# The last tile of the RWKV values' projection moved between the first pair's steps

## The chip, the cores and the metric

One NeuronCore of a Trainium2 chip runs the whole kernel. The metric is the device time of one execution in microseconds (us), lower is better. TensorE (PE in the rows) multiplies matrices, VectorE (DVE), ScalarE (ACT) and GpSimd (POOL) do the elementwise work, SyncE (SP) issues the transfers. Each engine takes its instructions in the order in which the program gives them, and waits at semaphores for the others.

## The reference

Two transformer blocks run one after the other on a sequence of 512 tokens with 1024 features, in float32. The change lies in the RWKV layer of the first block. Cut to what matters here:

```python
xr, xw, xk, xv, xa, xg = h[None] + xx[None] * mu[:, None, None, :]
r, k, v = jnp.einsum('nbsd,nde->nbse', jnp.stack([xr, xk, xv]), w_rkv)
w = -jax.nn.softplus(-(w0 + jnp.tanh(xw @ w1) @ w2)) - 0.5
a = jax.nn.sigmoid(a0 + (xa @ a1) @ a2)
g = jax.nn.sigmoid(xg @ g1) @ g2
...
y = _wkv7_scan(rh, decay, kh, vh, -kk, kk * ah)   # state = state*w + (state@a) b + v k
...
out = ((y + bonus).reshape(bsz, seq, d) * g) @ w_o
```

`_wkv7_scan` is a recurrence over the tokens for each of 16 heads of 64 features.

## The kernel before, in words

Activations stand transposed: 128 features of a tile on the partitions, 512 tokens along the row, 8 tiles. A float32 product is made of three products of rounded halves: weights' high with input's high (L697), weights' low with input's high (L698), weights' high with input's low (L703), each 128x128 by 128x512, for 8 blocks of the inner dimension. So a tile of a projection is 24 matmuls. The projections r, k and v run in this order, 8 tiles each; ScalarE copies each finished tile of v out of PSUM (L1261) into VV.

The scan is done in chunks of 64 tokens, and for a pair of heads (one tile of 128 features, "pair m", 8 pairs) at a time. Each pair has three kinds of step:

- "pre": 15 steps. Step 0 makes decay and rate products (TensorE L1519 and L1522) and their sigmoids (ScalarE L1617, L1620), then VectorE's running sum (L1683) and ScalarE's square (L1624); step 2 the column sums (L1529) and their reciprocal (VectorE L1688, L1690); steps 3 and 4 VectorE's L1693 to L1704 and ScalarE's exponentials; step 5 the decayed products (TensorE L1542, scaled by VectorE L1712, masked by GpSimd L1777); step 7 transposes the values (L1551, read twice by VectorE, L1718 and L1720, into VTOK); step 8 the keys' products (L1559, VectorE L1725); steps 10 to 12 further transposes and a product (L1567, L1573, L1580, L1587); step 13 the bonus (L1593, L1595); step 14 the gate (L1601 to L1608, copied by ScalarE L1667 to VV).
- "inv": the inverse of a triangular 64x64 matrix for each head and chunk: a first product (L1797, copied to TN by ScalarE L1830) and five levels. A level has a product u (L1806), VectorE's mask of it (L1839), two products (L1817 and L1823), and VectorE's two updates of TN and TT (L1844, L1847). The next level waits for them.
- "post": the state's recurrence over the 8 chunks and the output.

`rwkv_order` writes down in which order steps of the kinds of neighbouring pairs follow each other (pair m's inverse with pair m−1's post and pair m+1's pre), and `in_turn` runs this one list on every engine, so all queues have the same interleaving. Five steps of pair 0's pre are run between the tiles of v (AHEAD). The second weight of the gate (g2) is loaded by SyncE (L3188 and around), split by ScalarE (L1646, L1647) and VectorE (L1730, L1733) in pair 0's pre.

PSUM has 8 banks. In this phase they are rings that are handed out in the order of the same list: three banks for the inverse, ps3 to ps5 for pre and post, ps6, ps7 and ps5 for pair 0's first products. A product that takes a bank waits until its last user has been read.

## Time and profile before

| what | value |
|---|---|
| median of 3 runs | 2939.98 us |
| the three runs | 2934.58, 2939.98, 2943.99 us |
| the profiled execution | 2940.94 us, its span 2939.2 us |
| mean granted TensorE clock | 0.982 of full |
| TensorE busy | 2836.8 us, 97% of the span |
| VectorE, ScalarE, GpSimd busy | 1573.0, 1038.1, 189.2 us |

The span runs from the first to the last instruction of the profiled execution; the time holds what lies around it too. Times in the rows below count from the span's start. The stretch of this change begins near 738 us; the scan runs until about 1047 us.

### The profile page before, as it was taken

Reading aid. Unit: us, or ns where it says so; the run is one execution under the profiler, and the core shown is the slowest. Engines: PE = TensorE matmul, PEld = TensorE weight load, DVE = VectorE, ACT = ScalarE, POOL = GpSimd, SP = SyncE. Lnnn points to the kernel's source line nnn. Section 1 sums busy time; section 2 is a strip of 40 time slices with the busy share of each in tenths; the row PEclk is TensorE's granted clock in tenths of the full one; section 3 lists DMA queues with packets and bytes.
Section 4 is the critical chain, followed back from the end, with each engine's and each line's share of the span. In section 5 each row is a group of like instructions: output and inputs, shape, how many; then the busy total and the mean of one; then the engine's idle time right before and its main releaser. Section 6 shows DMA issues by size and latency. Waiting matters only on the chain.

```text
span 2939.2 us, 44934 instructions
## 1 busy us (share of the span) xinstructions
PE 2836.8 (97%) x20056; PEld 2296.9 (78%) x20056; DVE 1573.0 (54%) x2214; ACT 1038.1 (35%) x1338; POOL 189.2 (6%) x167
## 2 busy tenths in 40 slices
PE   7999999999899989999999999899999998999999
PEld 5878888778788878888777777688888786788887
DVE  7766544464677753233466666454344646454342
ACT  4235234353333235233432322242223447532221
POOL 0010000101322110000100000010000000100000
PEclk9999999999999999999999999799999999999999
DMA  7544554221000032222211111032322220222322
GB/s 276 227 172 174 199 200 171 81 86 44 17 3 3 17 115 101 100 101 93 76 58 44 44 44 44 1 115 78 116 92 88 91 82 1 89 98 79 115 83 68
DMA packets 41377, 270.78 MB, mean 92 GB/s; under 512 B 4576, under 2 KB 4832, under 8 KB 13280
## 3 DMA queue, kind: packets, MB, share of 16 engines
q1 hardware_dynamic: 40752, 266.37, 25.1%
q8 instruction: 157, 2.57, 0.3%
q10 hardware_dynamic: 432, 1.54, 0.1%
q14 instruction: 36, 0.29, 0.0%
HBM read 265.80 MB, written 2.10 MB: 91 GB/s over the span
## 4 chain that ended last, share of the span: by engine, by line
PE 88%; DVE 8%; ACT 3%; issue 1%; DMA 1%; SPq 0%; POOL 0%; DVEq 0%; ACTq 0%
PE ps L697 21%; PE ps L703 21%; PE ps L698 21%; PE ps L2276 6%; PE ps L3054 1%; PE ps L1823 1%; PE ps L1817 1%; PE ps L2382 1%; PE ps L1806 1%; PE ps L2441 1%; DVE WL L409 1%; PE ps L2435 1%; PE ps L2410 1%; PE ps L2971 1%; PE ps L2958 1%
## 5 line engine op out<-in xcount | busy, mean ns | idle before, releaser
L697 PE MATMUL ps<-HH,WH 128*128 128x512 f32 x1928 | 766.5, 398 | 19.4 <-ACT HH L673 16.6
L698 PE MATMUL ps<-HH,WL 128*128 128x512 f32 x1928 | 756.4, 392 | 0.0
L703 PE MATMUL ps<-HL,WH 128*128 128x512 f32 x1928 | 730.7, 393 | 4.9 <-DVE HL L909 3.6
L409 DVE TENSOR_TENSOR WL<-ST,WH 128x2048 fp32r<-128x2048 f32 (+3 forms) x230 | 465.1, 2023 | 230.8 <-ACT WH L401 230.7
L401 ACT ACTIVATE WH<-ST 128x2048 fp32r<-128x2048 f32 (+1 forms) x211 | 384.1, 1820 | 310.0 <-PE ps L703 281.6
L697 PEld LDWEIGHTS ps<-HH,WH 128*128 128x128 f32 x1928 | 365.4, 190 | 102.9 <-issue 23.5
L703 PEld LDWEIGHTS ps<-HL,WH 128*128 128x128 f32 x1928 | 364.5, 189 | 85.8 <-DVE HL L909 5.8
L698 PEld LDWEIGHTS ps<-HH,WL 128*128 128x128 f32 x1928 | 365.7, 190 | 78.6 <-issue 3.8
L698 PE MATMUL ps<-GH,WL 128*128 128x512 f32 x928 | 361.4, 389 | 0.0
L697 PE MATMUL ps<-GH,WH 128*128 128x512 f32 x928 | 361.4, 389 | 0.0
L703 PE MATMUL ps<-GL,WH 128*128 128x512 f32 x928 | 360.0, 389 | 0.0
L698 PEld LDWEIGHTS ps<-GH,WL 128*128 128x128 f32 x928 | 174.3, 188 | 36.2
L703 PEld LDWEIGHTS ps<-GL,WH 128*128 128x128 f32 x928 | 174.3, 188 | 36.1
L697 PEld LDWEIGHTS ps<-GH,WH 128*128 128x128 f32 x928 | 174.2, 188 | 36.0
L749 DVE SCALAR_TENSOR_TENSOR X<-ps,MOD,X 128x512 f32<-128x512 f32 (+1 forms) x52 | 36.3, 707 | 196.4 <-PE ps L703 196.4
L1016 DVE TENSOR_TENSOR GL<-TMP,GH 128x512 fp32r<-128x512 f32 x64 | 44.3, 692 | 169.0 <-ACT GH L1009 167.4
L532 POOL TENSOR_TENSOR ACC<-ACC,TMP 128x512 f32<-128x512 f32 x43 | 56.8, 1321 | 1059.9 <-ACT TMP L521 1050.8
L2276 PE MATMUL ps<-HH,WH 128*128 128x512 f32 x256 | 118.1, 461 | 0.0
L2276 PE MATMUL ps<-HL,WH 128*128 128x512 f32 x256 | 103.2, 403 | 0.0
L2276 PE MATMUL ps<-HH,WL 128*128 128x512 f32 x256 | 102.7, 401 | 0.0
L454 DVE CUSTOM_DVE_ANT_0 ADA<-ST,CROW,CC 128x1024 f32<-128x1024 f32 x80 | 102.5, 1318 | 0.0
L752 DVE TENSOR_TENSOR X<-X,ps 128x512 f32<-128x512 f32 x48 | 32.6, 685 | 129.7 <-PE ps L703 129.7
(408 smaller groups left out, 3519.0 us busy)
## 6 DMA issues: line engine op xcount, KB each, us to landing
ST<-w_m SPq DMA_DIRECT2D x64, 1024.0 KB, 4.8
ST<-w_gu SPq DMA_DIRECT2D x44, 1024.0 KB, 4.8
ST<-w_ada SPq DMA_DIRECT2D x40, 1024.0 KB, 5.7
ST<-w_dn SPq DMA_DIRECT2D x32, 704.0 KB, 4.1
ST<-w_gin SPq DMA_DIRECT2D x16, 1024.0 KB, 4.8
ST<-w_cin SPq DMA_DIRECT2D x12, 1024.0 KB, 4.9
ST<-w_rkv SPq DMA_DIRECT2D x12, 1024.0 KB, 4.8
W<-w_ada SPq DMA_DIRECT2D x16, 512.0 KB, 16.9
```

The lines of the kernel that those rows point to most:

```text
L401: e.activation(WH[:, j % 3, 0:n], ST[:, pos % 3, 0:n], ACT.Copy).then_inc(*hi.up(j))
L409: o = e.tensor_tensor(WL[:, j % 3, cut], ST[:, pos % 3, cut], WH[:, j % 3, cut].bitcast(F32), ALU.subtract)
L454: e.tensor_tensor_reduce(out=ADA[:, 2 * d:2 * d + 2, :], in0=tile, in1=CROW[:, :].rearrange("p (a b) -> p a b", a=2), scale=1.0, scalar=co ...
L532: e.tensor_tensor(sums_of(t)[:, :], sums_of(t)[:, :], tmp.tile(("square", t, k)), ALU.add).then_inc(*sumsq.up(t, k))
L697: e.matmul(ps[:, :], wh[:, k, cs], H[:, k, :], start=(k == 0), stop=False)
L698: e.matmul(ps[:, :], wl[:, k, cs], H[:, k, :], start=False, stop=False)
L703: o = e.matmul(ps[:, :], wh[:, k, cs], L[:, k, :], start=False, stop=(k == kt - 1))
L749: e.scalar_tensor_tensor(out=X[:, m, cs], in0=ps[:, cs], scalar=gcol(m), in1=X[:, m, cs], op0=ALU.mult, op1=ALU.add).then_inc(*res.up(tag, ...
L752: e.tensor_tensor(X[:, m, :], X[:, m, :], ps[:, :], ALU.add).then_inc(*res.up(tag, m))
L1016: e.tensor_tensor(GL[:, m, :], tmp.tile((tag, m)), GH[:, m, :].bitcast(F32), ALU.subtract).then_inc(*out_vec.up(tag, m))
L1806: o = e.matmul(ps[rows(hh), 64 * c:64 * c + 64], BG[b][rows(hh), c, 128:192], TN[rows(hh), c, :], start=True, stop=True)
L2276: o = e.matmul(ps[:, :], a[:, k, c0:c0 + P], b[:, k, :], start=(k == 0 and part == 0), stop=(k == KT - 1 and part == 2))
```

## The change

The last tile of v (tile 7) leaves the projection (`but=7`) and is made in eight steps of its own, kind "v", one for each block of the inner dimension, which `rwkv_order` puts between the steps 5 to 14 of pair 0's pre. Pair 1's pre step 0 comes before pair 0's bonus, in front of the inverse's first product; pair 0's gate product goes behind pair 1's step 8, and two of pair 1's steps behind the first level of the inverse. The split of the gate weights is now a kind of its own, "gates", two steps. Waits for tile 7 become waits for tile 6, and the instructions that need tile 7's end wait for it themselves; the load of g2 is issued behind tile 6.

```diff
@@ tensor_dense
-                for group in ([tiles] if n == 0 else [[m] for m in tiles]):
+                for group in ([tiles] if n == 0 else [[m] for m in tiles if m != but]):
@@ rwkv_order
-            out = [("pre", 0)] * PRE
+            a, b, v = ("pre", 0), ("pre", 1), ("v", 7)
+            out = [a] * AHEAD + [v, v, a, a, v, a, v, v, a, a, v, a, a, v, a, v, b, a, b]
...
-                    steps += [(moved("pre", i, PRE), 2, "pre", m + 1) for i in range(PRE)]
+                    steps += [(moved("pre", i, PRE), 2, "pre", m + 1) for i in range(0 if m else 2, PRE)]
                 steps = [(kind, n) for _, _, kind, n in sorted(steps)]
+                if m == 0:
+                    steps[3:3] = [steps.pop(2)]
+                    steps[13:13] = [a]
+                    steps[8:8] = [("gates", 0)]
+                    steps[5:5] = [("gates", 0)]
@@ scalar_pre
-                if m == 0 and i == 6:
-                    e.wait_ge(s_g2, 16)
-                    e.activation(G2H[:, :], LG2[:, 0, :], ACT.Copy).then_inc(*scan_act.up("g2 high"))
-                    e.activation(G2B, LG2[0:96, 1, :], ACT.Copy).then_inc(*scan_act.up("g2 tail"))
@@ vector_pre
+            if m == 1:
+                e.wait_ge(*mm.at("v", 7))
...
-            if m == 0:
-                e.wait_ge(*scan_act.at("g2 high"))
-                e.tensor_tensor(G2L[:, :], LG2[:, 0, :], G2H[:, :].bitcast(F32),
-                                ALU.subtract).then_inc(*scan_vec.up("g2 low"))
-                e.wait_ge(*scan_act.at("g2 tail"))
-                e.tensor_tensor(G2B[32:64, :], LG2[32:64, 1, :], G2B[32:64, :].bitcast(F32),
-                                ALU.subtract).then_inc(*scan_vec.up("g2 tail"))
@@ pool_pre
+            if m == 1:
+                e.wait_ge(*mm.at("v", 7))
+                e.tensor_tensor(RI[1][:, 0, :, :], over(tb("idk"), 8), over(tb("idk"), 8),
+                                ALU.mult).then_inc(*scan_pool.up("identity"))
@@ new functions
+        def tensor_value(e, m):
+            for k in range(KT):
+                tensor_group(e, "v", 3, [m], k, HH, HL, None, None, first_b)
+                yield
+
+        def scalar_value(e, m):
+            for k in range(KT - 1):
+                yield
+            e.wait_ge(*mm.at("v", m))
+            e.activation(VV[:, m, :], first_b.tile(("v", m))[:, :], ACT.Copy).then_inc(*out_act.up("v", m))
+            e.wait_ge(s_tab, 16)
+            e.activation(BONES, tb("bones"), ACT.Copy).then_inc(*scan_act.up("bones"))
+            yield
+
+        def scalar_gates(e, _):
+            e.wait_ge(*mm.at("v", 7))
+            e.wait_ge(s_g2, 16)
+            e.activation(G2H[:, :], LG2[:, 0, :], ACT.Copy).then_inc(*scan_act.up("g2 high"))
+            e.activation(G2B, LG2[0:96, 1, :], ACT.Copy).then_inc(*scan_act.up("g2 tail"))
+            while True:
+                yield
+
+        def vector_gates(e, _):
+            yield
+            e.wait_ge(*scan_act.at("g2 high"))
+            e.tensor_tensor(G2L[:, :], LG2[:, 0, :], G2H[:, :].bitcast(F32),
+                            ALU.subtract).then_inc(*scan_vec.up("g2 low"))
+            e.wait_ge(*scan_act.at("g2 tail"))
+            e.tensor_tensor(G2B[32:64, :], LG2[32:64, 1, :], G2B[32:64, :].bitcast(F32),
+                            ALU.subtract).then_inc(*scan_vec.up("g2 tail"))
+            while True:
+                yield
@@ tensor_rwkv (the other engines alike)
-            e.wait_ge(*out_act.at("v", 7))
+            e.wait_ge(*out_act.at("v", 6))
@@ SyncE
-                    e.wait_ge(*mm.at("v", 7))
+                    e.wait_ge(*mm.at("v", 6))
                     e.dma_start(LG2[:, :, :], lo2[:, 1:3, :]).then_inc(s_g2, 16)
```

The list of steps decides the rest, so here is what stands on the engines. Line numbers of the changed kernel are larger by 16 around the pre steps of TensorE (L1542 is L1558 there, L1551 is L1567, L1559 is L1575, L1519 is L1535) and by 11 in the inverse (L1806 is L1817, L1817 is L1828, L1823 is L1834).

TensorE before, at the end of the values' projection; the last three matmuls of tile 7 and pair 0's step 5:

```order
L697 MATMUL ps<-HH,WH 128x512
L698 MATMUL ps<-HH,WL 128x512
L703 MATMUL ps<-HL,WH 128x512
L1542 MATMUL ps<-RI_104,BP 64x128 [waits scan_pool,scan_vector,out_activated]
L1542 MATMUL ps<-RI_104,BP 64x128 x15
L1551 MATMUL ps<-TB,VV 128x128 x4
```

TensorE of the changed kernel at the same place; the first row is tile 7's first matmul:

```order
L697 MATMUL ps<-HH,WH 128x512 [waits out_activated]
L698 MATMUL ps<-HH,WL 128x512
L703 MATMUL ps<-HL,WH 128x512
L697 MATMUL ps<-HH,WH 128x512
L698 MATMUL ps<-HH,WL 128x512
L703 MATMUL ps<-HL,WH 128x512
L1558 MATMUL ps<-RI_104,BP 64x128 [waits scan_pool,scan_vector]
L1558 MATMUL ps<-RI_104,BP 64x128 x15
L697 MATMUL ps<-HH,WH 128x512
```

Tile 7 has two of its eight steps ahead of step 5 and six behind; tile 6's copy is what its first matmul waits for. This is TensorE of the changed kernel where tile 7 ends and pair 1 begins:

```order
L697 MATMUL ps<-HH,WH 128x512
L698 MATMUL ps<-HH,WL 128x512
L703 MATMUL ps<-HL,WH 128x512
L1535 MATMUL ps<-ADA,LO_81 128x512 [waits scan_vector]
L1538 MATMUL ps<-ADA,LO_81 128x512 [waits scan_activated]
L1609 MATMUL ps<-RKH,HH 128x512 [waits scan_activated]
L1611 MATMUL ps<-RKL,HH 128x512 [waits scan_pool]
L1808 MATMUL ps<-TB,TT_99 64x64 [waits scan_pool]
L1808 MATMUL ps<-TB,TT_99 64x64 x15
L1817 MATMUL ps<-TN,BG_89 64x64 [waits scan_activated]
L1817 MATMUL ps<-TN,BG_89 64x64 x15
L1828 MATMUL ps<-UN,TT_99 64x64 [waits scan_vector]
```

Pair 1's two products (L1535, L1538) and the bonus (L1609, L1611) stand ahead of the inverse's first product (L1808); before, the inverse's product stood ahead of pair 1's. The column sums (L1529, now L1545) were ahead of level 1's two products and are behind them.

VectorE before, first where the gate weights are split (L1730, L1733), in pair 0's pre:

```order
L1725 TENSOR_TENSOR GK_91<-ps,TB 128x4x128
L1730 TENSOR_TENSOR G2L<-LG_86,G2H 128x1024 [waits scan_activated]
L1733 TENSOR_TENSOR HL<-LG_86,HL 32x1024 [waits scan_activated]
L1736 TENSOR_TENSOR BG_89<-ps,TINY 128x8x64 [waits scan_summed]
L1740 TENSOR_TENSOR TT_99<-BG_89,TB_82 128x512 [waits scan_pool]
```

and then around the second level of pair 0's inverse (mask L1839, updates L1844 and L1847), with pair 1's L1712 between:

```order
L1704 SCALAR_TENSOR_TENSOR T_109<-RR,CC,KK 128x512 [waits scan_vector]
L1839 TENSOR_TENSOR UN<-ps,TB_82 128x512 [waits scan_summed]
L1712 TENSOR_TENSOR BG_93<-ps,TINY 128x4x128 [waits scan_summed]
L1844 TENSOR_TENSOR TN<-TN,ps 128x512 [waits scan_summed]
L1847 TENSOR_TENSOR TT_99<-TT_99,ps 128x512 [waits scan_summed]
```

VectorE of the changed kernel around the second level (mask L1850, gate weights L2078 and L2081, updates L1855 and L1858):

```order
L1850 TENSOR_TENSOR UN<-ps,TB_82 128x512 [waits scan_summed]
L1726 TENSOR_TENSOR BG_93<-ps,TINY 128x4x128 [waits scan_summed]
L2078 TENSOR_TENSOR G2L<-LG_86,G2H 128x1024 [waits scan_activated]
L2081 TENSOR_TENSOR HL<-LG_86,HL 32x1024 [waits scan_activated]
L1855 TENSOR_TENSOR TN<-TN,ps 128x512 [waits scan_summed]
L1858 TENSOR_TENSOR TT_99<-TT_99,ps 128x512 [waits scan_summed]
```

The two subtractions of the gate weights have gone from pair 0's pre to between the mask and the update of level 2.

TensorE before around the third level, with bank numbers: transposed values of pair 1, its keys' products, the level's two products:

```order
L1551 MATMUL ps4<-TB_58,VV_74 128x128 x4
L1559 MATMUL ps5<-RI1_105,KP_108 64x128 [waits scan_vector,scan_pool]
L1559 MATMUL ps3<-RI1_105,KP_108 64x128
...
L1817 MATMUL ps2<-UN_102,TT0_99 64x64 [waits scan_vector]
L1817 MATMUL ps2<-UN_102,TT0_99 64x64 x15
L1823 MATMUL ps0<-TT0_99,UN_102 64x64 x16
```

TensorE of the changed kernel at the same place:

```order
L1567 MATMUL ps3<-TB_58,VV_74 128x128 x4
L1575 MATMUL ps4<-RI1_105,KP_108 64x128 [waits scan_vector,scan_pool]
L1575 MATMUL ps3<-RI1_105,KP_108 64x128
...
L1617 MATMUL ps5<-GAH_78,G2H_88 128x512 [waits scan_activated]
L1619 MATMUL ps5<-GAL_79,G2H_88 128x512 [waits out_vector]
L1621 MATMUL ps5<-GAH_78,G2L_87 128x512
L1624 MATMUL ps5<-GBH_80,HL_51 128x512 [waits out_vector]
L1828 MATMUL ps2<-UN_102,TT0_99 64x64 x16
L1834 MATMUL ps0<-TT0_99,UN_102 64x64 x16
```

Pair 0's gate product (L1617 to L1624) now stands between the keys' products and the level's products. The transposed values are in ps3, which the keys' products use too; before they were in ps4, which these did not use.

## Rows read from the trace of the kernel before

**Rows 1.** The page: granted clock by slices, and the chain that ended last.
```profile
PEclk9999999999999999999999999799999999999999
...
PE 88%; DVE 8%; ACT 3%; issue 1%; DMA 1%; SPq 0%; POOL 0%; DVEq 0%; ACTq 0%
```

**Rows 2.** Time line, TensorE: start us, us, engine, line, operation, count, [idle before].
```profile
725.93 0.95 PE L1529 MATMUL ps<-TB,ACC 128*128 128x2 f32 x8
...
737.74 0.39 PE L697 MATMUL ps<-HH,WH 128*128 128x512 f32 x1
...
742.96 0.39 PE L703 MATMUL ps<-HL,WH 128*128 128x512 f32 x1
744.03 1.59 PE L1542 MATMUL ps<-RI,BP 64*64 64x128 f32 x32 [0.69 <-ACT VV L1261]
...
756.44 0.69 PE L1519 MATMUL ps<-ADA,LO 64*128 64x512 f32 x1
...
757.50 1.15 PE L1806 MATMUL ps<-TN,BG 64*64 64x64 f32 x32
```

**Rows 3.** Busy time by stretch; first a line of columns.
```profile
core 0: us, PE busy (x) PEld busy (x) DVE busy (x) ACT busy (x) POOL busy (x), PEclk, DMA share, GB/s
744.03:756.44 12.41, 9.43 (x150) 7.47 (x151) 8.99 (x12) 4.40 (x7) 6.06 (x5) 1.00 0.25 86
765.00:767.00 2.00, 2.00 (x38) 1.83 (x35) 1.62 (x3) 0.00 (x0) 1.50 (x2) 0.50 0.00 0
775.00:790.00 15.00, 14.87 (x345) 12.38 (x338) 8.96 (x15) 3.58 (x6) 2.73 (x3) 1.00 0.01 3
```

**Rows 4.** Time line, TensorE, pair 0's inverse.
```profile
761.60 1.05 PE L1529 MATMUL ps<-TB,ACC 128*128 128x2 f32 x8 [2.95 <-ACT ACC L1624]
762.58 1.15 PE L1817 MATMUL ps<-UN,TT 64*64 64x64 f32 x32
763.56 1.75 PE L1823 MATMUL ps<-TT,UN 64*64 64x64 f32 x32
...
772.40 1.15 PE L1806 MATMUL ps<-TN,BG 64*64 64x64 f32 x32
...
776.05 1.10 PE L1823 MATMUL ps<-TT,UN 64*64 64x64 f32 x32
...
782.71 1.15 PE L1806 MATMUL ps<-TN,BG 64*64 64x64 f32 x32
...
784.65 1.15 PE L1823 MATMUL ps<-TT,UN 64*64 64x64 f32 x32
```

**Rows 5.** Time line, VectorE.
```profile
727.70 0.69 DVE L1695 SCALAR_TENSOR_TENSOR KK<-ACC,KK 128x512 f32<-128x512 f32 x1
...
750.10 1.29 DVE L1730 TENSOR_TENSOR G2L<-LG,G2H 128x1024 fp32r<-128x1024 f32 x1
...
752.67 0.69 DVE L1736 TENSOR_TENSOR BG<-ps,TINY 128x512 f32<-128x512 f32 x1
...
766.81 0.69 DVE L1695 SCALAR_TENSOR_TENSOR KK<-ACC,KK 128x512 f32<-128x512 f32 x1
...
768.02 1.78 DVE L1704 SCALAR_TENSOR_TENSOR T<-RR,CC,KK 128x512 f32<-128x512 f32 x1
769.73 0.68 DVE L1839 TENSOR_TENSOR UN<-ps,TB 128x512 f32<-128x512 f32 x1
...
771.66 0.69 DVE L1844 TENSOR_TENSOR TN<-TN,ps 128x512 f32<-128x512 f32 x1 [0.65 <-PE ps L1817]
...
775.11 0.69 DVE L1720 SCALAR_TENSOR_TENSOR VTOK<-TINY,ps 128x512 f32<-128x512 f32 x1
...
783.90 0.69 DVE L1839 TENSOR_TENSOR UN<-ps,TB 128x512 f32<-128x512 f32 x1 [0.98 <-PE ps L1806]
```

**Rows 6.** Time line, GpSimd.
```profile
767.65 1.61 POOL L1773 TENSOR_TENSOR KP<-KK,TMP 128x512 f32<-128x512 f32 x1 [1.15 <-DVE KK L1695]
```

**Rows 7.** Source line L1704: duration ns min/median/max, first and last start.
```profile
L1704 DVE SCALAR_TENSOR_TENSOR T<-RR,CC,KK x8: 737/740/1794, 729.8 to 977.1; 128x512 f32<-128x512 f32 x8
```

More of the change, by code:

```diff
@@ L707, in tensor_group, with tensor_dense @@
                     o.then_inc(*took.up(tag, k))
-        def tensor_dense(e, tag, H, L, high, low, after=None, hooked=True, begun=(0,), norm=None, first=0):
+        def tensor_dense(e, tag, H, L, high, low, after=None, hooked=True, begun=(0,), norm=None, first=0, but=None):
             for n, j in enumerate(J[tag]):
@@ L1164, in plan_projections @@
                     for m in (2 * n, 2 * n + 1):
-                        big.use((tag, m), out_act, tag, m)
+                        if (tag, m) != ("v", 7):
+                            big.use((tag, m), out_act, tag, m)
             return ahead(plan_pre)
@@ L1219, in tensor_projections @@
                 tensor_dense(e, tag, HH, HL, split_high("mix" + tag), split_low("mix" + tag),
-                             lambda m: next(pre) if 1 < m < 2 + AHEAD else None, tag == "v")
+                             lambda m: next(pre) if 1 < m < 2 + AHEAD else None, tag == "v",
+                             but=7 if tag == "v" else None)
             return {("pre", 0): pre}
@@ L1259, in scalar_projections @@
                             scalar_split(e, "mix" + then, None, (tag, 7), tag)
+                        if (tag, m) == ("v", 7):
+                            continue
                         e.wait_ge(*mm.at(tag, m))
@@ L1506, in plan_wo, with plan_value @@
                 yield
+        def plan_value(m):
+            first_b.use(("v", m), out_act, "v", m)
+            while True:
+                yield
         def plan_rwkv(begun):
-            in_turn(RWKV, {"pre": plan_pre, "inv": plan_inv, "post": plan_post, "wo": plan_wo}, begun)
+            in_turn(RWKV, {"pre": plan_pre, "inv": plan_inv, "post": plan_post, "wo": plan_wo, "v": plan_value,
+                           "gates": no_value}, begun)
             plan_residual("wo", "mlp1")
@@ L1878, in tensor_post @@
             e.wait_ge(*scan_act.at("kt", m))
+            if m == 0:
+                e.wait_ge(*out_act.at("v", 7))
             if m:
@@ L2038, in scan_low, with no_value @@
             return scan_vec.at("low", k)
+        def tensor_value(e, m):
[25 more added lines that the diff above has]
+                            ALU.subtract).then_inc(*scan_vec.up("g2 tail"))
+            while True:
+                yield
+        def no_value(m):
+            while True:
+                yield
         def tensor_rwkv(e):
             begun = tensor_projections(e)
-            e.wait_ge(*out_act.at("v", 7))
+            e.wait_ge(*out_act.at("v", 6))
             in_turn(RWKV, {"pre": lambda m: tensor_pre(e, m), "inv": lambda m: tensor_inv(e, m),
-                           "post": lambda m: tensor_post(e, m), "wo": lambda n: tensor_wo(e, n)}, begun)
+                           "post": lambda m: tensor_post(e, m), "wo": lambda n: tensor_wo(e, n),
+                           "v": lambda m: tensor_value(e, m), "gates": no_value}, begun)
             tensor_dense(e, "wo", HH, HL, scan_high, scan_low, begun=(7,))
@@ L2057, in vector_rwkv @@
             begun = vector_projections(e)
-            e.wait_ge(*mm.at("v", 7))
-            e.wait_ge(*out_act.at("v", 7))
+            e.wait_ge(*mm.at("v", 6))
+            e.wait_ge(*out_act.at("v", 6))
             in_turn(RWKV, {"pre": lambda m: vector_pre(e, m), "inv": lambda m: vector_inv(e, m),
-                           "post": lambda m: vector_post(e, m), "wo": lambda n: vector_wo(e, n)}, begun)
+                           "post": lambda m: vector_post(e, m), "wo": lambda n: vector_wo(e, n),
+                           "v": no_value, "gates": lambda _: vector_gates(e, _)}, begun)
             vector_low(e, J["wo"][1])
@@ L2075, in pool_rwkv @@
                 next(begun["pre", 0])
-            e.wait_ge(*mm.at("v", 7))
-            e.wait_ge(*out_act.at("v", 7))
-            e.tensor_tensor(RI[1][:, 0, :, :], over(tb("idk"), 8), over(tb("idk"), 8), ALU.mult)
+            e.wait_ge(*mm.at("v", 6))
+            e.wait_ge(*out_act.at("v", 6))
             in_turn(RWKV, {"pre": lambda m: pool_pre(e, m), "inv": lambda m: iter(()), "post": lambda m: iter(()),
-                           "wo": lambda m: iter(())}, begun)
+                           "wo": lambda m: iter(()), "v": no_value, "gates": no_value}, begun)
             pool_squares(e, "mlp1")
```

7 lines of the change are left out of this document (3 added, 4 removed).

## The prediction, on record before the result

> **What bounds the kernel now.** I read the page first. The chain that ended last lies on TensorE for 88% of the span and on VectorE for 8% [rows 1]: what counts is when TensorE can start, and an edit gains only what it takes out of TensorE's gaps. Two numbers bound this edit. A tile of the values' projection is 24 matmuls, from 737.74 to 742.96 in starts, 0.227 us apart, so 5.44 us [rows 2]. And between the first step of pair 0 behind it (744.03) and the first of pair 1 (756.44) TensorE is busy for 9.43 of 12.41 us at the full clock [rows 2, 3]: 2.98 us are gaps. In front of 744.03 stand 0.69 us more, for ScalarE's copy of tile 7; a copy of tile 6 will be waited for in the same way, so that gap stays.
>
> Then I read on down TensorE's order of time. After 757.50 it stands for 2.95 us until 761.60, for ScalarE (table load, sigmoids, VectorE's scan, the square) [rows 4]. In 765 to 767 the granted clock is 0.50, the 1.2 GHz level; before it fell TensorE had been idle up to 761.60 and then ran 64-column matmuls [rows 3, 4]. From 775 to 790 it is busy for 14.87 of 15 us [rows 3]: what is late at 776.05, the second product of pair 0's third level, is late for good, and what is early there stays early. So 776.05 is the point at which I settle the account. Every later pair repeats an order of instructions that the change leaves alone.
>
> **The change, part by part.** The work is the same: no matmul, copy or transfer is added, the identity product on GpSimd only comes later. The sum is one of times.
>
> *1. The tile between pair 0's steps.* TensorE starts at 744.03 − 5.44 = 738.6, with two steps of the tile. To pair 1's first product (L1519) it then has the 9.43 us, less what is now put behind it: four gate matmuls (4 × 0.23 = 0.9), the two of the bonus (0.6) and the inverse's first product (about 1.0, the distance of two such groups at 762.58 and 763.56 [rows 4]), plus 5.44 of the tile: 9.43 − 2.5 + 5.44 = 12.4 us, to within half a us: L1519 at 751.0 for 756.44, so 5.4 earlier. The gaps are filled; VectorE's copies, for which they were, end behind the steps of the tile.
>
> *2. Pair 1's first steps.* Behind L1519 come ScalarE's table load and sigmoids, VectorE's scan and ScalarE's square, and TensorE could use the square 761.60 − 756.44 = 5.16 us behind L1519 [rows 2, 4], so at 756.2. ScalarE now does all this first and only then copies the inverse's first product (about 0.55 more, estimated from the other plain steps between engines here). The first level (L1806) starts at 756.7, against 757.50. Most of the 5.4 is gone here: the 2.95 us gap has moved ahead of L1806. The column sums (L1529), which waited for the square, now stand behind level 1: one level takes 1.94 to its second product (782.71 to 784.65), the two products about 1.0 each [rows 4]; so L1529 starts at 756.7 + 1.94 + 2.0 = 760.6. From L1529 to KK's update (L1695) pair 0 took 727.70 − 725.93 = 1.77 [rows 2, 5], and from there to level 2's mask (L1839) it is 769.73 − 766.81 = 2.92 [rows 5]. L1839: 760.6 + 1.77 + 2.92 = 765.3 for 769.73, 4.4 earlier.
>
> *3. The gate weights.* On VectorE L1730 and L1733 take 752.67 − 750.10 = 2.57 us [rows 5]. There they filled time in which TensorE stood anyway; now they stand directly ahead of level 2's update (L1844), for which level 3 waits on TensorE. L1844 follows L1839 by 1.93, of which the time line shows 0.65 idle, so by 1.28 of work; with the 2.57 it is 3.85: 769.15 for 771.66, 2.5 earlier. Then the port. The mask on GpSimd (L1777) now runs beside these two. KP's product on GpSimd (767.65, 1.61 us) and L1704 on VectorE (768.02, 1.78 us) overlap in this trace; L1704 reads two tiles of SBUF and takes 0.74 as a rule [rows 5 to 7]. If L1730 or L1733 is held in the same way, up to 1.05 is added; if GpSimd is the one held, nothing. Nearest is L1704, but here VectorE is first; I take 0.6. Left: 1.9 earlier at level 3 (772.40 becomes 770.5). ScalarE's two copies (G2H, G2B) cost nothing: it has no work between the exponentials and RKH. SyncE issues their load behind tile 6, not 7, and nothing is queued behind it until the gates of pair 7; GpSimd's identity product waits for tile 7 (751.2 in the new order) and takes GpSimd's place only while that waits for pair 1's sigmoids anyway.
>
> The Trainium skill (GPSIMD Engine Reference, section 1 Specifications) says that GpSimd's SBUF interfaces are shared with VectorE and that contention comes with instructions of two SBUF inputs. By that rule both gate subtractions are exposed and the full 1.05 would be due, 0.45 more than I take; L1704 agrees with it.
>
> *4. A new wait in the ring of PSUM tiles.* This is what the diff doesn't show and the order with tile numbers does: before, pair 1's transposed values go to ps4, and the decayed keys' product (L1559) to ps5 and ps3. Now both use ps3, so L1559 waits until VectorE has read the values twice (L1718, L1720). Before, L1720 started at 775.11, 2.7 behind level 3's start, and nobody waited. Now the mask on level 3's product (L1839) stands ahead, which starts 1.2 behind the product (782.71 to 783.90 [rows 4, 5]), then 0.6 of the mask, 0.7 of the sum L1718 and 0.7 of L1720 itself: L1559 can start 3.2 behind level 3. It then takes 1.5 (the like group at 744.03, 1.59 on its row, of which the last 0.1 lies under the next [rows 2]), the gate matmuls of pair 0, now behind it, 0.95 to 1.1, the first product 1.0. So the second product starts 6.75 behind level 3; before it was 776.05 − 772.40 = 3.65. That is 3.1 later.
>
> **Sum:** 1.9 earlier at level 3, 3.1 later behind it: 1.2 us later at 776.05, and as much at the end. Against the profiled execution (2940.94, of which 2939.2 is span) this gives 2942.1; its time is 1 us above the median of the three runs, 2939.98, so by the median **2941.2 us**. Bounds: without the port (−0.6), with the gate matmuls at 0.9 and L1559's tail beside the next group (−0.7) it is −0.1; with the full port (+0.45) and half the clock for one level's products, which took 1.75 for 1.15 at 763.56 [rows 4] and would now touch column sums too (+1.2), it is +2.9. This case's own range is 2939.9 to 2942.9, to which the runs' scatter, 2934.58 to 2943.99, is to be added.
>
> **Rivals.**
> (a) *The gain is kept.* If L1559 doesn't wait for L1720 in effect, or the gate subtractions slip into VectorE's idle time, 2 to 5.4 us stay: 2934.5 to 2938. For it: 2.98 us of gaps are really filled. Against: the order on VectorE is fixed, and the tile numbers are. It decides at level 3: this case needs it over 3.1 us earlier. Chance 0.27, middle 2937.
> (b) *TensorE's clock.* Level 1 to 3 now has gaps of about 2.8, 0.7, 1.1, 1.0 and 1.6 us in 20. If the whole of it runs at 1.2 GHz, some 8.6 us of products on the path (two a level, sums, keys, gates) take twice as long: 2941.2 + 8.6 = 2950, slower by over 0.3%. Against: 0.50 was granted here for some 3 us only. It decides when over 7.5 us of the products are at half clock. Chance 0.06 for that much.
> (c) *The clock elsewhere.* The page's PEclk shows a slice at 7 behind the middle [rows 1]: far from the change, and 0.3 of a slice of 73.5 us is some 22 us of clock. A shift by a few us may change its length either way. If a third of it goes, 2934; half, 2930. Chance 0.12, split over both signs.
> The Trainium skill (TensorE: Matmul & The Clock Gate, "Why this matters for your kernels") advises against idle gaps between bursts because the clock falls back. By that rule (b) would be likelier before than after, since the longest gap is 2.95 and would be about 2.8; no run here yet shows it.
>
> **How the numbers follow.** Forecast (0 to 3 us slower) 0.55, (a) 0.27, (b) 0.06, (c) 0.12. A measurement of this kernel can tell about 0.3%, 8.8 us, from no change; neither the forecast nor (a) reaches that, since the tile's 5.44 us are the most that can be had. So within 0.3%: 0.55 + 0.27 + most of (c) = 0.89; slower by more 0.06, from (b); faster by more 0.05, from (c). The range 2935 to 2946 holds the forecast and (a) with part of the scatter.
>
> **What the profile after would show.** L1542's first group at about 738.6 + 1.5; L1519 of pair 1 at 751.0; L1806 at 756.7 behind a wait for TN of nearly 3 us; the level 2 update on VectorE directly behind L1733's row, at 769 to 770; L1559 of pair 1 with a wait of 1 to 2 us for VTOK; L1823 of level 3 at 776 to 778.5. I am wrong if L1559 doesn't wait there, if level 3 starts before 769, or if the time from there to the end of the scan differs from that of before.

## The result and the profile after

The changed kernel takes **2946.74 us** (median of 22 runs, 2938.09 to 2957.99) and the kernel before 2939.26 us (22 runs, 2933.21 to 2944.74). The medians differ by 7.5 us. The ratio over all runs is 1.0031, with a 95% interval of 1.0023 to 1.004: slower by 0.31%. The forecast was 2941.2, in a range of 2935 to 2946; the median lies just above it. The profiled execution of the changed kernel took 2945.96 us, of which 2944.2 are its span, 5.0 us more than that of before.

The page of the changed kernel gives the first hint, against [rows 1]:

```profile
PEclk9999999999899999999999999799999999999999
...
PE 88%; DVE 8%; ACT 3%; issue 1%; DMA 1%; SPq 0%; DVEq 0%; ACTq 0%
```

TensorE still holds 88% of the chain. In the middle a slice of PEclk stands at 7 in both. But there is a new 8, the eleventh slice, that is 736 to 810 us: just where the change is. The time line of TensorE of that stretch, with the columns of [rows 2]:

```profile
750.03 0.69 PE L1535 MATMUL ps<-ADA,LO 64*128 64x512 f32 x1
...
755.68 1.98 PE L1817 MATMUL ps<-TN,BG 64*64 64x64 f32 x32 [2.77 <-ACT TN L1841]
758.45 1.97 PE L1828 MATMUL ps<-UN,TT 64*64 64x64 f32 x32 [0.79 <-DVE UN L1850]
...
765.28 2.61 PE L1558 MATMUL ps<-RI,BP 64*64 64x128 f32 x30 [1.10 <-DVE RI L1715]
...
772.97 1.97 PE L1817 MATMUL ps<-TN,BG 64*64 64x64 f32 x32 [2.78 <-DVE TN L1855]
...
777.58 2.89 PE L1575 MATMUL ps<-RI,KP 64*64 64x128 f32 x32 [1.60 <-DVE VTOK L1734]
780.40 0.79 PE L1617 MATMUL ps<-GAH,G2H 128*128 128x512 f32 x1
...
783.40 1.10 PE L1834 MATMUL ps<-TT,UN 64*64 64x64 f32 x32
```

I read it against [rows 2, 4]. Everything is counted from tile 6's last matmul, 737.51 before and 736.71 now, so that what happened earlier in the execution drops out.

| from tile 6's last matmul, us | before | after | forecast of the difference | measured |
|---|---|---|---|---|
| pair 1's first product (L1519, now L1535) | 18.93 | 13.32 | −5.4 | −5.61 |
| level 1 starts (L1806, now L1817) | 19.99 | 18.97 | −0.8 | −1.02 |
| level 3 starts | 34.89 | 36.26 | −1.9 | +1.37 |
| level 3's second product (L1823, now L1834), called D below | 38.54 | 46.69 | +1.2 | +8.15 |
| last copy of the scan on ScalarE, called S below | 304.89 | 312.90 | as D | +8.01 |

Up to level 1 the forecast holds to 0.2 us. Then 2.4 us come on until level 3, and 6.8 in level 3. From there to the end of the scan nothing changes any more (8.15 and 8.01). In the rows one sees why: L1817 (L1806 before) took 1.15 and takes 1.98 at 755.68 and 1.97 at 772.97; L1828 (L1817 before) takes 1.97 at 758.45 for 1.15, and L1575 2.89 at 777.58, for the 1.59 of the like group at 744.03. The granted clock of the changed kernel, by stretches (the columns are those of [rows 3]):

```profile
core 0: us, PE busy (x) PEld busy (x) DVE busy (x) ACT busy (x) POOL busy (x), PEclk, DMA share, GB/s
...
750.00:755.00 5.00, 2.90 (x39) 1.61 (x38) 1.92 (x2) 3.88 (x7) 2.11 (x2) 1.00 0.00 0
755.00:760.00 5.00, 3.53 (x61) 3.34 (x62) 0.69 (x1) 4.97 (x8) 2.37 (x3) 0.52 0.01 3
760.00:765.00 5.00, 4.18 (x80) 3.91 (x78) 3.17 (x7) 0.09 (x1) 0.81 (x2) 0.80 0.00 0
765.00:770.00 5.00, 4.72 (x96) 4.72 (x96) 4.32 (x5) 0.63 (x1) 2.41 (x2) 0.66 0.02 5
770.00:775.00 5.00, 2.22 (x41) 1.97 (x36) 4.07 (x5) 0.00 (x0) 1.93 (x2) 0.72 0.00 0
775.00:780.00 5.00, 3.40 (x34) 3.03 (x36) 2.06 (x3) 0.00 (x0) 1.68 (x2) 0.50 0.02 3
...
738.00:790.00 52.00, 42.96 (x684) 36.34 (x683) 27.50 (x39) 13.36 (x21) 17.79 (x13) 0.80 0.07 22
```

Two of the same stretches of the kernel before:

```profile
775.00:780.00 5.00, 5.00 (x149) 4.71 (x142) 4.59 (x9) 0.60 (x1) 1.47 (x2) 1.00 0.01 3
738.00:790.00 52.00, 43.40 (x806) 36.13 (x806) 29.53 (x43) 16.64 (x26) 16.74 (x13) 0.97 0.07 22
```

The clock is full until 755. Level 1 runs at 0.52 (the 1.2 GHz level), then it is mixed from 760 to 775, and from 775 to 780 it is at 0.50 again. Read in stretches of half a microsecond, it is at the low level three times: from about 755.2 to 762.0, 765.4 to 768.8 and 772.2 to 782.5. Ahead of each TensorE stood idle: 2.77 us before 755.68, for TN, 1.10 us before 765.28, for RI, and 2.78 us before 772.97, for TN again. Over the 52 us it was granted 0.80 for 0.97. It was busy about as long (42.96 and 43.40 us) with 684 instructions instead of 806, so it got less done in the same busy time. The ends of matmuls are modelled, so busy time alone does not show this; the starts do.

VectorE and GpSimd around the gate weights, against [rows 5, 6]:

```profile
768.78 1.22 DVE L2078 TENSOR_TENSOR G2L<-LG,G2H 128x1024 fp32r<-128x1024 f32 x1
770.03 2.17 DVE L2081 TENSOR_TENSOR HL<-LG,HL 32x1024 fp32r<-32x1024 f32 x1
772.22 0.69 DVE L1855 TENSOR_TENSOR TN<-TN,ps 128x512 f32<-128x512 f32 x1
```

```profile
768.94 2.17 POOL L1788 TENSOR_TENSOR BG<-BG,TB 128x512 f32<-128x512 f32 x1 [2.59 <-DVE BG L1726]
774.19 1.27 POOL L1788 TENSOR_TENSOR BG<-BG,TB 128x512 f32<-128x512 f32 x1 [3.07 <-DVE BG L1726]
```

The first subtraction takes 1.22, the second 2.17 us. Together they last from 768.78 to 772.22, 3.44 us for the 2.57 of before. GpSimd's mask beside them needs 2.17 instead of the 1.27 that it takes at 774.19. That is the contention for which the forecast took 0.6. By the starts and ends the two engines look as if they took turns: the mask starts 0.16 behind the first subtraction, which takes its usual time (1.22, and 1.29 before), and ends 1.11 behind that one's end; the second subtraction ends 1.09 behind the mask's end.

### The profile page after: what moved, and what is told of

It is laid out like the page before. It is cut to its first block, busy times and chain, and to the rows that moved or that the text cites. A ratio compares the mean times of both kernels' runs of the same rounds, so it can differ in the third digit from the quotient of the medians.

```text
span 2944.2 us, 44934 instructions
## 1 busy us (share of the span) xinstructions
PE 2840.9 (96%) x20056; PEld 2299.9 (78%) x20056; DVE 1574.0 (53%) x2214; ACT 1037.9 (35%) x1338; POOL 190.4 (6%) x167
## 3 DMA queue, kind: packets, MB, share of 16 engines
q8 instruction: 157, 2.57, 0.4%
## 4 chain that ended last, share of the span: by engine, by line
PE 88%; DVE 8%; ACT 3%; issue 1%; DMA 1%; SPq 0%; DVEq 0%; ACTq 0%
PE ps L697 21%; PE ps L703 21%; PE ps L698 21%; PE ps L2326 6%; PE ps L3104 1%; PE ps L1834 1%; PE ps L1828 1%; PE ps L1817 1%; PE ps L2432 1%; PE ps L2491 1%; DVE WL L409 1%; PE ps L2485 1%; PE ps L2460 1%; PE ps L3021 1%; PE ps L3008 1%
```

## The experiments

Each kernel ran 12 times, in turn with the kernel before (median 2939.2 to 2939.5 in all three comparisons); the last was run once. D and S are defined above and come from one profiled execution each. "Rest" is the span less the end of the scan, so the part of the program in which no kernel here differs from another. "Clock" is the granted clock of 738 to 790 us.

| kernel | median (range), us | ratio to before, 95% | D | S | clock | rest |
|---|---|---|---|---|---|---|
| before | 2939.26 (2933.21 to 2944.74) | | 38.54 | 304.89 | 0.97 | 1896.8 |
| changed | 2946.74 (2938.09 to 2957.99) | 1.0031, 1.0023 to 1.004 | 46.69 | 312.90 | 0.80 | 1894.6 |
| e1_fill_after | 2939.15 (2932.14 to 2943.78) | 1.0, 0.9989 to 1.0011 | 40.25 | 306.66 | 1.00 | 1893.0 |
| e2_fill_before | 2940.32 (2933.79 to 2948.03) | 1.0008, 0.9994 to 1.0022 | 38.68 | 304.99 | 1.00 | 1894.0 |
| e3_ring | 2944.32 (2935.08 to 2954.08) | 1.0014, 0.9999 to 1.0029 | 42.59 | 310.03 | 0.84 | 1904.4 |
| e4_gates | 2941.79 (2932.31 to 2949.57) | 1.0008, 0.9996 to 1.0021 | 40.74 | 307.00 | 0.90 | 1904.3 |
| e5_inv_first | 2942.8 (2932.53 to 2954.88) | 1.0014, 1.0 to 1.0028 | 40.86 | 307.21 | 0.93 | 1894.0 |
| e6_all | 2934.88 (2930.48 to 2940.89) | 0.9986, 0.9975 to 0.9997 | 36.44 | 303.98 | 0.93 | 1890.8 |
| e7_reorder | 2936.89 (2932.9 to 2943.59) | 0.9992, 0.9981 to 1.0003 | 35.02 | 304.39 | 0.93 | 1890.6 |
| e8_fill_first | 2940.79 (2935.16 to 2954.37) | 1.0002, 0.9986 to 1.0017 | 40.16 | 306.46 | 1.00 | 1904.3 |
| e9_tile_only | 2942.28 (2937.96 to 2949.89) | 1.0015, 1.0003 to 1.0028 | 42.08 | 308.49 | 0.90 | 1890.6 |
| e10_all_fill | 2941.03 (2933.75 to 2945.09) | 1.0003, 0.9992 to 1.0014 | 35.67 | 303.15 | 1.00 | 1904.3 |
| e11_fill_rest | 2942.4 (2934.04 to 2945.17) | 1.0003, 0.9992 to 1.0015 | 42.81 | 309.15 | 0.93 | 1895.8 |
| e12_again | 2936.84 (one run) | | 45.02 | 311.21 | 0.87 | 1887.8 |

The rest varies by 17 us between executions and hides what the order is worth, so a median can tell the changed kernel from before but hardly the experiments from each other. What the stretch costs is read from D and S. Two rows show where the rest gets its differences, 1500 to 1900 us of e6_all and then of e10_all_fill:

```profile
1500.00:1900.00 400.00, 386.78 (x3631) 275.89 (x3625) 255.00 (x552) 116.90 (x174) 14.08 (x14) 0.95 0.11 38
```

```profile
1500.00:1900.00 400.00, 388.88 (x3544) 277.90 (x3540) 249.30 (x538) 115.83 (x171) 14.07 (x14) 0.91 0.11 38
```

The granted clock is 0.95 in one and 0.91 in the other, of 400 us; 0.04 of 400 is 16 us of clock, against 13.5 us in the rest.

### The clock or the order

**e1_fill_after** puts products that compute nothing into TensorE's gaps: matmuls of HH into a bank that nobody reads then. They keep TensorE running and change nothing else of the work.

```diff
+        def tensor_fill(e, n):
+            for _ in range({1: 12, 2: 3, 3: 4, 4: 8, 5: 6}[n]):
+                e.matmul(PY[:, :], HH[:, 1, 0:P], HH[:, 2, :], start=True, stop=True)
+            while True:
+                yield
...
+                    for at_, n in ((14, 5), (12, 4), (8, 3), (2, 2), (1, 1)):
+                        steps[at_:at_] = [("fill", n)]
```

> The changed kernel with 33 dummy matmuls (128x512, read from two unused places of HH, written to a free PSUM bank) in TensorE's five gaps between pair 0's first inverse product and pair 1's keys' products: 12, 3, 4, 8 and 6 of them. They do no useful work and wait for nothing. Measure D: from tile 6's last matmul to the second product of level 3, 38.5 us before, 46.7 in the changed kernel. Theory (clock): the order of instructions costs about 1 us, the other 7 are TensorE at 1.2 GHz between the gaps; with the gaps filled the granted clock stays near 1.00, D is 39.5 to 41.5 and the time about 2941, 5 to 7 us under the changed kernel. Rival (order): the new waits themselves cost it; D stays at 45 or more (the dummies can only add) and the time at 2946 or more.

TensorE's level 3 in e1_fill_after, and its clock:

```profile
773.33 1.59 PE L1577 MATMUL ps<-RI,KP 64*64 64x128 f32 x32 [0.22 <-DVE VTOK L1736]
...
776.96 1.10 PE L1836 MATMUL ps<-TT,UN 64*64 64x64 f32 x32
```

```profile
738.00:790.00 52.00, 50.41 (x835) 40.68 (x836) 30.00 (x43) 15.38 (x25) 17.91 (x13) 1.00 0.06 22
```

The clock is full over the whole stretch, and D is 40.25 for 46.69. So **6.4 of the 8.15 us are the clock, and 1.7 are the order.** The median says the same: 2939.15, 7.6 below the changed kernel and within its interval equal to before; the intervals of the two ratios (0.9989 to 1.0011 and 1.0023 to 1.004) don't meet. More work on TensorE, 33 matmuls of 128x512, made the changed kernel faster.

**e2_fill_before** does the same to the kernel before, so that its own 0.50 in 765 to 767 [rows 3] goes.

```diff
+                if m == 0:
+                    for at_, n in ((10, 4), (9, 3), (4, 1)):
+                        steps[at_:at_] = [("fill", n)]
```

(12, 4 and 3 matmuls in fills 1, 3 and 4.)

> The kernel before with 19 such dummy matmuls in its own gaps there: 12 before pair 1's column sums (the 2.95 us gap), 4 and 3 in the two gaps of about 1 us at 767 and 770. Theory (clock): the stretch at half clock from 763 to 767 vanishes; on the path that was one product of 1.5 for 0.95 us, so D goes from 38.5 to 37.5 to 38 and the time down by 0.5 to 1 us, which is less than these rounds can tell; the profile decides. Rival (order): D stays 38.5 or grows by what the dummies overrun.

The clock is 1.00 for 0.97, and D stays: 38.68 for 38.54. The gain of 0.5 to 1 us that I expected does not come. The rows of VectorE and GpSimd show why, first of before, then of e2_fill_before:

```profile
765.31 1.19 POOL L1768 TENSOR_TENSOR RI<-RR,T 128x512 f32<-128x512 f32 x1
765.95 0.82 DVE L1693 TENSOR_SCALAR ACC<-XX,CC 128x512 f32<-128x512 f32 x1
```

```profile
764.75 1.20 POOL L1775 TENSOR_TENSOR RI<-RR,T 128x512 f32<-128x512 f32 x1
764.75 1.48 DVE L1700 TENSOR_SCALAR ACC<-XX,CC 128x512 f32<-128x512 f32 x1
```

Counted from the column sums (761.60 and 761.03), VectorE comes to this step 0.63 us earlier at full clock. But beside GpSimd's product it now takes 1.48 us for 0.82, and ends 0.3 us behind GpSimd's end in both kernels. So the half clock was on the path for 0.6 us, and GpSimd's product would have held VectorE in its place. The clock of before has nothing to give back at this place, and that of the changed kernel has.

### Which gap

**e8_fill_first** fills only the gap ahead of level 1, with 12 matmuls; **e11_fill_rest** all but that one (3, 4, 10 and 6).

```diff
# e8_fill_first
+                    steps[1:1] = [("fill", 1)]
# e11_fill_rest
+                    for at_, n in ((14, 5), (12, 4), (8, 3), (2, 2)):
+                        steps[at_:at_] = [("fill", n)]
```

> The changed kernel with 12 dummy matmuls in the first gap alone (2.77 us, behind the inverse's first product). Theory (each long gap lets the clock fall again): the clock stays 1.00 to about 770 and falls behind the second gap of 2.78 us ahead of level 3, so that level 3's product, keys' and gate products keep their half clock; D 43 to 44.5, time 2943 to 2945. Rival (the first gap alone starts it): D about 40.5, time 2941, as with all gaps filled.

TensorE in e8_fill_first (L2095 is the fill), and its clock:

```profile
751.99 3.02 PE L2095 MATMUL ps<-HH 128*128 128x512 f32 x12
754.94 1.15 PE L1818 MATMUL ps<-TN,BG 64*64 64x64 f32 x32
...
769.07 1.15 PE L1818 MATMUL ps<-TN,BG 64*64 64x64 f32 x32 [2.56 <-DVE TN L1856]
...
772.42 1.59 PE L1576 MATMUL ps<-RI,KP 64*64 64x128 f32 x32 [1.62 <-DVE VTOK L1735]
...
776.06 1.10 PE L1835 MATMUL ps<-TT,UN 64*64 64x64 f32 x32
```

```profile
765.00:770.00 5.00, 2.44 (x84) 2.30 (x80) 4.94 (x5) 0.00 (x0) 2.18 (x1) 1.00 0.00 0
...
738.00:790.00 52.00, 45.09 (x817) 36.61 (x817) 29.98 (x43) 15.53 (x25) 17.85 (x13) 1.00 0.05 20
```

The clock stays full, though two gaps are left, 2.56 and 1.62 us, and TensorE is busy for 2.44 us only in 765 to 770. My expectation, that each gap takes the clock down on its own, was wrong for this execution. What differs from the changed kernel is that TensorE had not been at half clock before. That is no explanation, though. In e5_inv_first (below) the clock was at 0.50 until 765.6, TensorE stood idle for 3.01 us from 767.2, and it came back at full clock:

```profile
770.24 1.15 PE L1818 MATMUL ps<-TN,BG 64*64 64x64 f32 x32 [3.01 <-DVE TN L1856]
```

And in e6_all and e7_reorder (below too) the clock was full from 750 on and fell at a later gap, of 2.85 and 3.06 us.

Since here nothing is slowed, this profile also shows the order by itself: level 3 starts at 769.07, 33.17 behind tile 6's last matmul (735.90), 1.7 earlier than before, and its second product is 6.99 behind it. The forecast had 1.9 and 6.75.

> The changed kernel with all its gaps filled but the first, the counterpart of e8_fill_first, where the first alone was filled and the clock stayed at 1.00 (D 40.2) although gaps of 2.56 and 1.62 us were left. Theory formed from that (the first gap, behind which the first level's small products come, is what the clock answers): low clock from about 755 for some 6 us, D 42 to 44. Rival (any of the gaps does it, and e8_fill_first's one profile was lucky): also low behind the first gap, but then e8's median should not be as good as e1's, and D here is about 42 all the same; what tells them apart is whether the second half (770 to 782) stays at 1.00 here.

TensorE in e11_fill_rest, and its clock:

```profile
754.72 1.97 PE L1819 MATMUL ps<-TN,BG 64*64 64x64 f32 x32 [2.77 <-ACT TN L1843]
...
774.93 1.59 PE L1577 MATMUL ps<-RI,KP 64*64 64x128 f32 x32 [0.22 <-DVE VTOK L1736]
...
778.56 1.10 PE L1836 MATMUL ps<-TT,UN 64*64 64x64 f32 x32
```

```profile
755.00:760.00 5.00, 5.00 (x69) 4.13 (x68) 0.69 (x1) 4.11 (x6) 2.41 (x2) 0.50 0.02 3
...
765.00:770.00 5.00, 4.29 (x99) 3.81 (x96) 4.97 (x5) 0.63 (x1) 2.90 (x2) 1.00 0.02 5
...
775.00:780.00 5.00, 5.00 (x116) 4.37 (x118) 1.67 (x3) 0.60 (x1) 0.32 (x1) 1.00 0.01 3
```

The gap of 2.77 us is back, and behind it the clock is at 0.50 for one stretch, full after 765. D is 42.81, 2.6 more than with all gaps filled. So in these profiles the first gap costs 2.6 of the 6.4 us, and the later low stretches 3.9. Among the changed kernel, e8_fill_first and e11_fill_rest they came only where the first gap and their own were open together. With one profile of each kernel this does not show that they need both.

**e12_again** is the changed kernel once more, in a single run.

> The changed kernel once more, for one look: whether the half clock recurs at the same places. Theory (the fall is caused by the gaps): low again in most of 755 to 782, D 44 to 48. Rival (a chance of the one profile): 1.00 there, D about 40.

Level 3 in e12_again, and its clock:

```profile
771.73 1.61 PE L1817 MATMUL ps<-TN,BG 64*64 64x64 f32 x32 [2.57 <-DVE TN L1855]
```

```profile
770.00:775.00 5.00, 2.65 (x36) 2.13 (x36) 4.12 (x6) 0.00 (x0) 2.04 (x2) 0.72 0.00 0
```

The clock in 755:760 is 0.51 again, in 770:775 0.72 and in 775:780 0.60; only 765:770, 0.66 in the first profile, is at 1.00. D is 45.02, 1.7 less. The low stretches at level 1 and level 3 come again, the one at level 2 does not. So the same instructions with the same gap of 1.10 us ahead of level 2 ran at half clock in one execution and at full clock in the other. And ahead of level 3 the clock had been full since 762.0 when the gap of 2.57 us began at 769.2, and it fell all the same (at 772.2, 0.5 us behind the gap's end), while in e8_fill_first it held over 2.56. The two differ in the low stretch at level 1, but by e5_inv_first, e6_all and e7_reorder that does not decide either. Each profile is one case of something that varies. Its whole time is 2936.84, 10 below the median, although its D is bad: the rest is 1887.8, the shortest of all.

### Which part of the change makes the gaps

Each undoes one part in the order of steps.

```diff
# e3_ring: the gate product behind pair 1's step 8, out of level 3
-                    steps[13:13] = [a]
+                    steps[15:15] = [a]
# e4_gates: the gate weights early, in level 1
-                    steps[8:8] = [("gates", 0)]
-                    steps[5:5] = [("gates", 0)]
+                    steps[2:2] = [("gates", 0)]
+                    steps[1:1] = [("gates", 0)]
# e5_inv_first: the inverse's first product ahead of pair 1's step 0
-            out = [a] * AHEAD + [v, v, a, a, v, a, v, v, a, a, v, a, a, v, a, v, b, a, b]
+            out = [a] * AHEAD + [v, v, a, a, v, a, v, v, a, a, v, a, a, v, a, v, ("inv", 0), b, a, b]
+                    steps.pop(0)
```

> The changed kernel with pair 0's gate product two steps later (behind pair 1's step 9), so that the banks are handed out otherwise and pair 1's keys' products no longer use the bank of its transposed values. The wait of 1.60 us for VTOK goes. Rival (order): D 46.7 becomes 44.5 to 45.1, the wait and up to half a us of the gate product. Theory (clock): the same and more, since one gap fewer lets the clock return earlier: keys' products and gate product took 4.8 us at half clock for 2.5; D 42 to 44.5, time 2942 to 2945.

> The changed kernel with the split of the gate weights earlier: ScalarE's two copies behind the copy of the inverse's first product, VectorE's two subtractions behind level 1's mask, instead of between level 2's mask and its update. Level 2's update then follows its products; the gap of 2.78 us before level 3 shrinks to under 0.5. Rival (order): D 46.7 becomes 43 to 44 (2.57 of subtractions and 0.95 of port less, 0.5 more at level 1). Theory (clock): the same and also the clock of level 3, keys' and gate products (about 4 us lost there) back: D 39 to 41.5, time 2939 to 2942.

> The changed kernel with the inverse's first product ahead of pair 1's first products, as in the kernel before, so that ScalarE copies it before it loads its table, and level 1's product needn't wait for pair 1. D (tile 6's last matmul to level 3's second product) was 38.5 before, 46.7 in the changed kernel, 40.25 with its gaps filled. Theory (the 2.77 us gap ahead of level 1 lets the clock fall, order costs 1.7 us in all): the gap goes, level 1 starts 3 us earlier, D 37.5 to 41, time 2936 to 2941. Rival (the clock falls in any case in this stretch of small products, whatever the order): D 43 or more, time 2943 or more.

Level 3 in e3_ring:

```profile
774.16 1.97 PE L1817 MATMUL ps<-TN,BG 64*64 64x64 f32 x32 [2.77 <-DVE TN L1855]
...
777.11 2.25 PE L1575 MATMUL ps<-RI,KP 64*64 64x128 f32 x26
...
780.51 1.10 PE L1834 MATMUL ps<-TT,UN 64*64 64x64 f32 x32
781.53 0.50 PE L1617 MATMUL ps<-GAH,G2H 128*128 128x512 f32 x1
```

and in e4_gates:

```profile
769.74 1.15 PE L1817 MATMUL ps<-TN,BG 64*64 64x64 f32 x32
...
773.28 1.59 PE L1575 MATMUL ps<-RI,KP 64*64 64x128 f32 x32 [1.81 <-DVE VTOK L1734]
...
776.92 1.10 PE L1834 MATMUL ps<-TT,UN 64*64 64x64 f32 x32
```

e3_ring: the keys' product (L1575) starts 2.95 behind level 3 and waits for nothing, for 4.61 in the changed kernel, and the gate product (L1617) stands behind the level. The second product comes 6.35 behind level 3 instead of 10.43, and D is 4.1 less. So the wait for VTOK does hang on the gate product's place in the ring. The gap of 2.77 us ahead of level 3 stays, and with it the low clock at its start. e4_gates: the gap ahead of level 3 is gone, and the products of level 3 run in 1.15 and 1.10. GpSimd's mask no longer runs beside the two subtractions there: the second takes 1.22 for 2.17, and the mask 1.27 for 2.17. The product of GpSimd that now overlaps the second one (L1776) takes 1.85 for its 1.27. So the contention moves along with what runs side by side. The wait for VTOK stays at 1.81. D is 5.95 less. e5_inv_first: the wait ahead of level 1 is gone, one of 2.21 us for VectorE's mask comes a product later, and D is 5.8 less. In all three D lies where the clock theory had it (42 to 44.5, 39 to 41.5, 37.5 to 41). None of the three is resolved by its median from before (1.0008 to 1.0014).

**e9_tile_only** moves only the tile. Pair 1's steps stand as before, and the gate weights are split as early as tile 7 allows.

```diff
+            out = [a] * AHEAD + [kinds[c] for c in "vvaavavvaavaavavGaGa"]
+                    steps = [kinds[c] for c in "ibbibibbibibibbibibbibibib"]
```

(a and b are pre steps of pair 0 and 1, v the tile, G the gate weights, i the inverse.)

> One part alone: tile 7's steps between pair 0's steps as in the changed kernel, but the gate weights split directly behind tile 7, the gate product and everything of pair 1 in the order of the kernel before. D is 38.5 before and 46.7 in the changed kernel. Theory (the split can't start before tile 7 has read its inputs, so that the tile's 5.4 us of cover come back as a wait for the gate weights in front of the gate product): TensorE waits some 3 us there, D 38 to 40 at full clock and up to 43 if the clock falls behind that wait, time 2939 to 2944. Rival (the tile alone brings its 3 us of gaps): D 35.5 to 36.5, time 2936 to 2937.

D is 42.08, 3.5 worse than before, although the 5.44 us of the tile fill the gaps. The split of the gate weights overwrites HL, which tile 7 still reads, so it can only come behind tile 7. TensorE then waits 0.97 us ahead of the bonus, for ScalarE's copies behind tile 7, and 1.04 and 0.84 us in the gate product, for the two subtractions: 2.85 us, where the gaps of before were 2.98. So the gap that the tile fills comes back behind it. The wait ahead of the column sums stays (2.65 us for 2.95). The clock is at 0.90 in that stretch, so a part of the 3.5 is the clock again; how much, no run with fills tells. The ratio, 1.0015 (1.0003 to 1.0028), says slower too.

### The three together, and the best order

**e6_all** has the edits of e3, e4 and e5 at once; **e7_reorder** is an order written by hand, with the inverse as early as it can go; **e10_all_fill** is e6_all with 9, 4 and 11 matmuls of fill (the 4 and the 11 came to stand together, ahead of level 2).

```diff
# e7_reorder
+            out = [a] * AHEAD + [kinds[c] for c in "vvaavavvaavaavavibaib"]
+                    steps = [kinds[c] for c in "ibbGibibbGibbibaibbibibib"]
# e10_all_fill, on e6_all
+                    for at_, n in ((7, 3), (6, 2), (3, 1)):
+                        steps[at_:at_] = [("fill", n)]
```

> The inverse's first product ahead of pair 1 (as e5), the gate weights split early (as e4) and the gate product behind step 9 (as e3), together. Theory (each gap is removed where it arises): D 34 to 38, clock mostly 1.00 from 751 to 785, time 2934 to 2939. Rival (clock falls anyway): D 40 or more.

> As e6, but pair 1's scan behind level 1's mask on VectorE, level 2's product and mask ahead of its two last exponent products, and VectorE's gate subtractions behind both of pair 1's decayed products. Theory: the inverse's chain runs ahead of pair 1's, D 33 to 37, time 2933 to 2938. Rival (pair 1's own chain of ScalarE, VectorE and GpSimd bounds the stretch): D within 0.5 of e6's.

> e6_all with dummy matmuls in its three remaining gaps (9 ahead of level 1's two products, 4 ahead of level 2, 11 ahead of pair 1's decayed products). e6_all had D 36.4 with the clock at 0.54 in 765 to 770. Theory (the clock is what e6_all still loses): D 35 to 36, time 2934 to 2935. Rival (its gaps are too few for the clock to cost): D 36.4 or more.

TensorE in e6_all:

```profile
757.03 1.15 PE L1829 MATMUL ps<-UN,TT 64*64 64x64 f32 x32 [2.21 <-DVE UN L1851]
...
765.27 2.68 PE L1559 MATMUL ps<-RI,BP 64*64 64x128 f32 x30 [2.85 <-DVE RI L1716]
...
774.01 1.10 PE L1835 MATMUL ps<-TT,UN 64*64 64x64 f32 x32
```

Level 1 has moved into the time of the sigmoids, and its second product (L1829) waits 2.21 us there. D is 36.44, 2.1 less than before, and S 0.9 less. The median, 2934.88, is 12 us below the changed kernel and the only one whose interval lies below 1 (0.9975 to 0.9997, 1 to 7 us faster than before); 0.9 (by S) to 2.1 us (by D) of that are the stretch's, what is left may be the rest's. e7_reorder has the best D, 35.02, and gives back part of it by S (304.39). e10_all_fill has a clock of 1.00 and the best S, 303.15, but a median of 2941.03, where I had expected 2934 to 2935. Its profiled rest is 13.5 us longer than that of e6_all. Whether the fills bring this about, or chance, stays open.

## Why the prediction was wrong

*Part 1, the tile: right.* L1535 came 5.6 us earlier against 5.4.

*Part 2, pair 1's first steps: right.* L1817 waits 2.77 us for TN, "nearly 3" as forecast, and level 1 starts 1.0 earlier against 0.8. That the gap only moves was right; what it does to the clock at its new place was missed. Before, the clock fell behind that gap too, for the last product of level 1 and the first of level 2, and that cost nothing in the end (e2_fill_before). Now level 1's first product follows the gap directly, and all of level 1 ran at the low level.

*Part 3, the gate weights: right in size.* The contention added 0.95 us (L2081 at 2.17 against 1.22), where I took 0.6 of 0 to 1.05. It held both engines, since GpSimd's mask also took 0.9 longer; I had thought of it as one or the other. It did not slow the first subtraction (1.22). By their starts the two subtractions together last 0.87 longer than before. The Trainium skill (GPSIMD Engine Reference, section 1 Specifications) calls these interfaces shared and names two SBUF inputs as a cause; the trace agrees for the second subtraction and the mask, and the full 1.05 is nearer than my 0.6.

*Part 4, the ring: right.* L1575 waits 1.60 us for VTOK. At full clock (e8_fill_first) the second product is 6.99 behind level 3, against 6.75, and 3.65 before.

*The sum for the order: right.* It was +1.2; e1_fill_after measures D at +1.7 with the clock at 1.00, e8_fill_first at +1.6. The parts agree as well as the total, so this is not luck.

***The step that failed is the clock.*** The sum took the whole stretch at 2.4 GHz, and had "half the clock for one level's products" as a bound only, at +1.2. Rival (b), which priced it at +8.6 and gave 2950, got a chance of 0.06 with the argument "0.50 was granted here for some 3 us only". The runs showed +6.4, about three quarters of (b). The argument was bad in two ways. First, the length of the low stretch of before was no measure of what would come. e2_fill_before shows that this one cost nothing in the end, and the changed order is another one: its account had five gaps, of 2.8, 0.7, 1.1, 1.0 and 1.6 us, all in the 20 us in which the small products of three levels stand on the path. Second, I priced the length of the gaps and not what they do to the products behind them. Four of the five had the right size (2.77, 0.79, 1.10 and 1.60 measured). The one ahead of level 3 was 2.78, and 2.56 at full clock in e8_fill_first, where I wrote 1.0: the start of level 3 was worked out along VectorE, rightly, but the gap that TensorE has there was not, though the two subtractions stand in it.

The Trainium skill (TensorE: Matmul & The Clock Gate, "Why this matters for your kernels") advises against idle gaps between bursts. I read it as a sign that (b) was likelier before than after, since the longest gap was 2.95 before. The trace shows the reverse, 0.97 before and 0.80 after, so the length of the longest gap did not decide. Nor does it in the other kernels: full clock followed 3.01 us (e5_inv_first), half clock 2.57 us (e12_again) and, in the first profile of the changed kernel, 1.10 us. The rule as advice agrees with e1_fill_after.

*Rivals (a) and (c).* (a) is out, since the order costs 1.7 even at full clock. (c) is real as scatter: the rest of one and the same kernel was 1894.6 and 1887.8 in two profiles. It does not explain the result, because D and S carry it.

*The size that is left:* the medians differ by 7.5 us; the stretch shows 8.15 in one profile and 45.02 − 38.54 = 6.5 in the other, 7.3 in the mean. So the share of the clock varies between executions: with the order at 1.7 it is 6.4 us in one and 4.8 in the other.

*What stays open:* what decides whether the clock falls at a given gap, since it held over 2.56 us in e8_fill_first and 3.01 us in e5_inv_first and fell at 1.10 us in one profile of the changed kernel and not in the other; and what sets the clock in 1500 to 1900 us.

## What to carry to other kernels

When an edit turns one long gap into several short ones ahead of small products that depend on each other, price the products behind the gaps at 1.2 GHz as well. If they stand on the path, count that as a likely case and not only as the bound: of the profiles here with an unfilled gap of over 2 us, all but e8_fill_first had the low clock somewhere in the stretch. Test for it cheaply: put matmuls that compute nothing into the gaps. They cannot shorten a wait, so what the stretch gets shorter by was the clock. And look at what stands beside a product that a faster clock would end earlier: in e2_fill_before a step of VectorE beside GpSimd's took the gain back. Last, a piece of work that fills a gap takes along everything that needs it done (here the split of the gate weights, behind the tile that still read HL), so ask what is late behind the filler before counting the gap as gained.
